# Half-size inverse matrices in a chunked delta rule, the first token group ahead of value and bonuses, and gate products issued inside the last group's norm

## The reference

```python
def wkv7_scan(r, decay, k, v, a_vec, b_vec):        # the delta rule: 8 heads of 64 x 64
    def step(S, inp):
        r_t, w_t, k_t, v_t, a_t, b_t = inp
        sa = jnp.einsum('bhij,bhj->bhi', S, a_t)
        S = (S * w_t[:, :, None, :] + sa[..., None] * b_t[:, :, None, :]
             + v_t[..., None] * k_t[:, :, None, :])
        return S, jnp.einsum('bhij,bhj->bhi', S, r_t)
...
    y = ((y - mean) * lax.rsqrt(var + LNX_EPS)).reshape(bsz, L, RWKV_WIDTH) * lnx_w + lnx_b
    bonus = jnp.sum(rh * kh * r_k, axis=-1, keepdims=True) * vh
    y = (y + bonus.reshape(bsz, L, RWKV_WIDTH)) * g
...
    _, states = lax.associative_scan(s5_combine, (a_elems, bu), axis=1)   # the diagonal model
    y = jnp.real(jnp.einsum('gcp,blgp->blgc', c, states)) + d.astype(f32).reshape(S5_GROUPS, S5_GROUP) * ug
    y = jax.nn.gelu(y.reshape(bsz, L, S5_WIDTH)).astype(u.dtype)
    return y * jax.nn.sigmoid(y @ w_glu + b_glu)
```

## Time and profile before

| | us |
|---|---|
| median of 3 runs | 3404.6 (3401.97 to 3408.07) |
| profiled execution, its own time | 3403.58 |
| its span, first to last instruction | 3402.0 |
| PE busy in the span | 3243.2 (95%) |
| DVE / ACT / POOL busy | 1505.4 / 813.5 / 858.6 |
| mean granted PE clock | 0.986 of full speed |

### The profile page before, as it was taken

How to read it: one execution, slowest core, us unless ns; L and a number is a source line. 1 busy time by engine, 2 the same in 40 slices (tenths; PEclk the granted TensorE clock), 3 DMA queues, 4 the chain that set the end, 5 groups by cost and what they waited for, 6 DMA issues and landing times. The chain is left out here.

```text
span 3402.0 us, 39434 instructions
## 1 busy us (share of the span) xinstructions
PE 3243.2 (95%) x15294; PEld 2320.1 (68%) x15294; DVE 1505.4 (44%) x2685; ACT 813.5 (24%) x1798; POOL 858.6 (25%) x537
## 2 busy tenths in 40 slices
PE   8999999999999999999999999989799999999998
PEld 7857767764444686776666544457587766888886
DVE  5574502331111565646654111143687632655552
ACT  3363301021111344432321111122222121211100
POOL 4314112310000430311003100014255231353352
PEclk9999999999999999999999999999899999999999
DMA  4351221147888322022232688871101122122221
GB/s 154 120 221 50 83 91 75 50 173 288 324 320 309 130 86 88 26 99 106 99 136 99 248 319 324 324 265 75 71 29 54 60 90 99 50 75 95 79 99 50
DMA packets 54206, 470.77 MB, mean 138 GB/s; under 512 B 5888, under 2 KB 10368, under 8 KB 30592
## 3 DMA queue, kind: packets, MB, share of 16 engines
q1 hardware_dynamic: 29040, 379.00, 30.2%
q0 software_dynamic: 21136, 78.39, 5.9%
q10 hardware_dynamic: 3840, 10.75, 0.8%
HBM read 506.65 MB, written 63.18 MB: 167 GB/s over the span
## 5 line engine op out<-in xcount | busy, mean ns | idle before, releaser
L662 PE MATMUL bank<-B,ring 128*128 128x256 f32 x4080 | 900.0, 380 | 17.3 <-DVE B L781 4.4
L662 PEld LDWEIGHTS bank<-B,ring 128*128 128x128 f32 x4080 | 775.7, 191 | 134.7 <-issue 28.4
L646 POOL TENSOR_TENSOR ring<-ring 128x1024 f32<-128x1024 f32 x58 | 148.7, 2563 | 1209.1 <-DMA ring<-in_w_static 378.6
L2095 PE MATMUL bank<-ring,B 128*128 128x512 f32 x960 | 419.1, 594 | 0.3
L812 ACT ACTIVATE B<-bank 128x256 f32<-128x256 f32 x384 | 145.0, 382 | 1022.2 <-PE bank L662 1020.0
L662 PE MATMUL bank<-XT,ring 128*128 128x256 f32 x1472 | 335.2, 382 | 18.9 <-DMA ring<-in_w_static 10.0
L2095 PEld LDWEIGHTS bank<-ring,B 128*128 128x128 f32 x960 | 180.2, 190 | 218.8 <-issue 218.8
L662 PEld LDWEIGHTS bank<-XT,ring 128*128 128x128 f32 x1472 | 280.5, 191 | 64.8 <-issue 17.3
L550 PE MATMUL bank<-B,ring 128*128 128x512 f32 x704 | 305.6, 592 | 4.6 <-DVE B L1496 3.5
L550 PEld LDWEIGHTS bank<-B,ring 128*128 128x128 f32 x704 | 133.5, 190 | 166.0 <-issue 163.9
L2170 DVE TENSOR_TENSOR B<-B,bank 128x512 f32<-128x512 f32 x46 | 31.6, 688 | 468.4 <-PE bank L2095 407.7
(11 more groups left out here) (526 smaller groups left out, 4094.1 us busy)
## 6 DMA issues: line engine op xcount, KB each, us to landing
ring<-in_w_expert SPq DMA_DIRECT2D x96, 2048.0 KB, 9.2
ring<-in_w_static SPq DMA_DIRECT2D x78, 2048.0 KB, 8.5
B<-in_w_expert SPq DMA_DIRECT2D x42, 2048.0 KB
slots_y<-B POOLq DMA_DIRECT2D x52, 512.0 KB, 27.9
B<-slots_x POOLq DMA_DIRECT2D x44, 512.0 KB
slots_x<-B POOLq DMA_DIRECT2D x23, 512.0 KB, 16.2
ring<-s_tables SPq DMA_DIRECT2D x4, 2048.0 KB, 8.4
s_tables<-tmp POOLq DMA_DIRECT2D x8, 512.0 KB, 3.3
```

The costliest lines, as they stand in the source:

```text
L646: pool.tensor_tensor(s(0), w(1, 0), w(1, 1), ALU.add).then_inc(made.up(), 1)
L662: ins = pe.matmul(out, left, right, start=start and k == 0, stop=k == 3, skip_group_check=not start)
L2095: ins = pe.matmul(bank[:, :], xbT[q % 2][:, k, :], slot[:, k, :], start=k == 0, stop=k == KT - 1)
```

## The change

- The inverse uses that chunks of 32 never leave a half of 64 tokens: each head's matrix is kept as two 64 x 64 blocks, one on partitions 0 to 63 and one on 64 to 127. All 8 heads fit one bank. `blockwise` makes 16 products of 64 x 64 where two banks had 4 of 128 x 128 each; squares alternate between two pairs of buffers. L and its transpose share a bank for each `par` (`half_gram`), so does MkT; `mv` and `u` work by halves.
- V is turned in round 2 and not ahead of the round. The shifts of V and the bonuses, `values_and_bonuses`, run in group 0's rounds on DVE; ACT first copies the bonus sums from their banks. Step 1 of the diagonal model moves into group 0, and the steps behind it by two places, so that groups 0 to 3 hold three, four, four and four.
- In pass 4 PE ends the diagonal model's outputs behind chain step 1, ACT makes the gelu there, and the 16 gate matmuls are issued as 3 + 2 + 2 + 9 around the products of the last norm in place of held-clock products. `h_kept` is loaded in group 3.

```diff
+        "above_eye": np.concatenate([near & (at < col), at == col], 1),
         "chunk_upper_incl": same & (i[:, None] <= i[None, :]),
     }
     c = np.stack([tables[n] for n in CONST_NAMES], 1).astype(np.float32)
 
     A, Bh, Kh, Rh = kk, a, k, r
...
-    M, MT, TTr = pair(m.B[0], 4), pair(m.B[0], 6), pair(m.XT, 0)
-    MkT, W1, U = pair(m.XT, 2), pair(m.XT, 4), pair(m.XT, 6)
+    tokB, tokK, tokV = [m.B[0][:, 0, :], m.tmp[:, 3, :]], [m.B[0][:, 1, :], m.rt[:, :]], [m.B[0][:, 2, :], m.XT[:, 2, :]]
+    by_head = lambda t: t.rearrange("p (h i) -> p h i", i=64)
+    fresh = m.B[0][:, 4:6, :].rearrange("p k (h i) -> p k h i", i=64)
+    power = [(fresh[:, 0], fresh[:, 1]), (by_head(m.B[0][:, 6, :]), by_head(m.B[0][:, 7, :]))]
+    MkT, TTr = by_head(m.XT[:, 0, :]), by_head(m.XT[:, 1, :])
+    W1, U = pair(m.XT, 4), pair(m.XT, 6)
...
-    grams = {"L": (A, Bh), "LT": (Bh, A), "MkT": (Kh, A), "NbT": (Bh, Rh), "NkT": (Kh, Rh)}
+    half_grams = {"L": ((A, Bh), (Bh, A)), "MkT": ((Kh, A),)}
+    grams = {"NbT": (Bh, Rh), "NkT": (Kh, Rh)}
...
-                for name in "ABKV":
+                for name in "ABK":
                     plan("tok", tg, name)
-                for name in ("LT", "L"):
-                    for par in range(2):
-                        plan(name, tg, par)
+                for par in range(2):
+                    plan("L", tg, par)
...
                 if tg < TT:
-                    for par in range(2):
-                        if rnd < 4:
-                            plan("sq", tg, rnd, par)
-                        if rnd < 3:
-                            plan("sqT", tg, rnd, par)
-                        if rnd > 0:
-                            plan("tt", tg, rnd, par)
+                    if rnd < 4:
+                        plan("sq", tg, rnd)
+                    if rnd < 3:
+                        plan("sqT", tg, rnd)
+                    if rnd > 0:
+                        plan("tt", tg, rnd)
...
+                if tg < TT and rnd == 2:
+                    plan("tok", tg, "V")
...
+            if tg == TT:
+                plan("glu", 3)
...
-        for j in range(CT):
-            bk.plan(("glu", j), (4, 5)[j % 2])
+        for j in range(3):
+            bk.plan(("glu", j), (*BU_BANKS, SY_BANK)[j])
...
-            feed()
...
+            def half_gram(name, tg):
+                for par in range(2):
+                    pe.wait_ge(*bk.vacant((name, tg, par)))
+                for i, (left, right) in enumerate(half_grams[name]):
+                    for ct in range(4):
+                        for b in range(2):
+                            t, at = slice(tg * P + 64 * b, tg * P + 64 * b + 64), i * 256 + 64 * ct
+                            for par in range(2):
+                                ins = pe.matmul(bk.bank((name, tg, par))[rows(b), at:at + 64], left[rows(par), ct, t], right[rows(par), ct, t],
+                                                start=True, stop=True)
+                                if (i, ct, b) == (len(half_grams[name]) - 1, 3, 1):
+                                    ins.then_inc(bk.full_sem((name, tg, par)), 1)
+
+            def blockwise(key, left, right):
+                pe.wait_ge(*bk.vacant(key))
+                out = by_head(bk.bank(key)[:, :])
+                for head in range(8):
+                    for b in range(2):
+                        ins = pe.matmul(out[rows(b), head, :], left[rows(b), head, :], right[rows(b), head, :], start=True, stop=True)
+                ins.then_inc(bk.full_sem(key), 1)
...
+            def square_round(tg, rnd):
                 if rnd == 0:
...
+                    pe.wait_ge(*bk.vacant(("sq", tg, 0)))
+                    hold_clock(m, pe, bk.bank(("sq", tg, 0)), 7)
+                    pe.wait_ge(*bk.read_done(("L", tg, 0)))
+                    pe.wait_ge(*bk.read_done(("L", tg, 1)))
...
+                M, MT = power[rnd % 2]
                 if rnd < 4:
...
+                    blockwise(("sq", tg, rnd), MT, M)
...
+                    blockwise(("sqT", tg, rnd), M, MT)
...
+                        pe.wait_ge(*bk.read_done(("tt", tg, rnd - 1)))
+                    blockwise(("tt", tg, rnd), M, TTr)
...
+            def gate_products():
+                pe.wait_ge(*m.landed(("glu", 0, 0)))
+                pe.wait_ge(*m.tally("s5_gelu").at(4))
+                for j in range(CT):
+                    pe.wait_ge(*bk.vacant(("glu", j)))
+                    for kt in range(CT):
+                        ins = pe.matmul(bk.bank(("glu", j))[:, :], glu_w[:, kt, j * P:(j + 1) * P], u[:, kt, :], start=kt == 0, stop=kt == CT - 1)
+                        if kt == CT - 1:
+                            ins.then_inc(bk.full_sem(("glu", j)), 1)
+                        yield
+
+            gate_calls = gate_products()
+
+            def fill(n):
+                for _ in range(n):
+                    next(gate_calls, None)
...
                 pe.wait_ge(*bk.vacant(("gm", tg)))
-                if tg == TT - 1:
-                    hold_clock(m, pe, bk.bank(("gm", tg)), 3)
...
-                hold_clock(m, pe, bank, 5)
+                if tg == TT - 1:
+                    fill(2)
+                else:
+                    hold_clock(m, pe, bank, 5)
...
-                    if rnd in (1, 3):
+                    if tg < TT and (rnd == 3 or rnd == 1 and tg):
...
+                        square_round(tg, rnd)
...
+                    if (tg, rnd) == (TT, 1):
+                        for _ in track:
+                            pass
                     if tg < TT:
-                        if rnd < 3:
-                            gram(("MkT", "NbT", "NkT")[rnd], tg)
+                        if rnd == 0:
+                            half_gram("MkT", tg)
+                        if rnd in (1, 2):
+                            gram(("NbT", "NkT")[rnd - 1], tg)
+                        if rnd == 2:
+                            if tg == 0:
+                                pe.wait_ge(*m.tally("shifted_tile").at(len(SHIFTED)))
+                            turned(tg, "V", v)
...
-                                at = (par * 4 + ct) * 64
-                                ins = pe.matmul(bank[:, at:at + 64], MkT[:, par, ct, :], tokV[tg % 2][:, hcol(par, ct)], start=True, stop=True)
+                                head = par * 4 + ct
+                                for b in range(2):
+                                    ins = pe.matmul(bank[rows(b), head * 64:head * 64 + 64], MkT[rows(b), head, :], tokV[tg % 2][rows(b), hcol(par, ct)],
+                                                    start=True, stop=True)
...
+                if tg == TT:
+                    fill(3)
...
+                    pe.wait_ge(*bk.read_done(("tt", tg, 4)))
...
-                            ins = pe.matmul(bank[:, ct * P:(ct + 1) * P], TTr[:, par, ct, :], W1[:, par, ct, :], start=True, stop=True)
+                            for b in range(2):
+                                ins = pe.matmul(bank[rows(b), ct * P:(ct + 1) * P], TTr[rows(b), 4 * par + ct, :], W1[rows(b), par, ct, :],
+                                                start=True, stop=True)
...
-            for _ in track:
-                pass
-            pe.wait_ge(*m.landed(("glu", 0, 0)))
-            pe.wait_ge(*bk.vacant(("glu", 0)))
-            hold_clock(m, pe, bk.bank(("glu", 0)), 7)
...
-                project(m, pe, ("glu", j), lambda kt, c: glu_w[:, kt, c * P:(c + 1) * P], j, CT, lambda kt: u[:, kt, :])
+            fill(4 * CT)
...
+            for j in range(CT):
+                evict(("bo", j), bonus[:, j, :], lambda b: b[:, :])
...
+                        M, MT = power[(rnd + 1) % 2]
+                        if rnd == 1:
+                            act.wait_ge(*m.tally("first_inverse").at(tg + 1))
+                        evict(("sq", tg, rnd), M, lambda b: by_head(b[:, :]))
+                        if rnd < 3:
+                            evict(("sqT", tg, rnd), MT, lambda b: by_head(b[:, :]))
+                        if rnd == 2:
+                            evict(("tok", tg, "V"), tokV[tg % 2], lambda b: b[:, :])
...
+                    if tg == TT - 1:
+                        act.dma_start(m.B[0][:, :, :], m.dram["h_kept"]).then_inc(m.restored, 16)
...
+                if tg == TT:
+                    for c in range(4):
+                        act.wait_ge(*bk.read_done(("sy", c)))
+                        act.activation(u[:, c, :], u[:, c, :], ACT.Gelu_apprx_tanh).then_inc(m.tally("s5_gelu").up(), 1)
+                    act.activation(m.v[:, 63:64], m.small[:, ROW_EPS], ACT.Sqrt)
...
-            act.dma_start(m.B[0][:, :, :], m.dram["h_kept"]).then_inc(m.restored, 16)
             act.dma_start(m.XT[:, :, :], m.dram["x_kept"]).then_inc(m.restored, 16)
-            for c in range(4):
...
-            shift(3)
-            dve.wait_ge(*m.tally("shifted_tile").at(len(SHIFTED)))
...
-            for j in range(CT):
-                dve.wait_ge(*bk.made(("bo", j)))
```

(54 more changed lines are left out.)

103 lines of the change are left out of this document (32 added, 71 removed).

## The result

The changed kernel takes 3377.0 us (median of four runs, 3373.4 to 3380.6) against 3404.8 (3402.0 to 3408.1, four runs): a ratio of 0.9918, 95% interval 0.9901 to 0.9935. The forecast was 3371, with 3352 to 3394 as its range. The profiled execution took 3373.7 us.

The account below looks back on a forecast made before the run. PE's order of work sets the pace in groups 0 to 3, DVE nearly so, DVE before them, a chain of small steps at the end: -19.4 - 7.5 - 7.5 - 6.9 + 14.3 - 6.3 = -33.3, giving 3371 us, range 3352 to 3394.

Parts of the forecast that it names:

- 1. The rounds, and group 3: Groups 1 to 3: smaller products and less DVE work save 7.5 us each in groups 1 and 2, 6.9 in group 3.
- 2. The start: Ahead of and in group 0: transposes start 18.1 us earlier, group 0 itself gains 1.3, so group 1 starts 19.4 earlier.
- 3. The clock: Sign against the forecast, in the groups' rounds: it would be wrong if PE's granted clock there is below 1.
- rival (e): Rounds: the half-empty array lets PE's clock fall, slower; 3437 us if half the new work runs at half speed; chance 0.08.
- 4. What is late next: Last chain and outputs: PE waits about 5.8 us for POOL's late end of step 15; +14.3 us in all (8 to 18).
- the low clock: Last chain: after PE's gap for POOL, some 6 us of work at half speed, +2.9 us.
- the stall of 1.8: Last chain: a second weight transfer can hold PE's instructions as in group 3, half of 3.6, +1.8 us.
- 5. The tail: After the last outputs: gate products issued around the norm's products cut 24.8 us to 18.5, a gain of 6.3.
- (b): Small things go well: no stall or low clock in the last chain, faster small products, group 3 without gap; 3356 us; chance 0.15.
- (c): DVE becomes the bound: three groups save 5.2 in place of 7.5, group 0 saves 7 less; 3385 us; chance 0.13.
- (d): Small products run one behind the other, `blockwise` 1.76 us, so the rounds gain nothing on PE; 3398 us; chance 0.05.
- the other signs that were to show the forecast wrong: No DVE waits in groups 1 to 3, V tiles at 3.3 us each, or DVE closing the last chain's gap early.

Follow-up runs that it names:

- e5: Changed kernel with value and bonuses back ahead of group 0 and the gate products back behind the last norm, leaving chiefly the half-size matrices: 3376.1 us.
- e1: Changed kernel with the state's sum kept in PSUM, so the multiplication by the decay reads one SBUF input: 3368.3 us.
- e6: Changed kernel with only the move of value and bonuses undone: they come ahead of group 0 again, gates stay moved: 3370.4 us.
- after: The changed kernel itself, with the whole change and no further edit: 3377.0 us.
- e2: Changed kernel with POOL's six products of a diagonal-model step on 8 columns in place of 512, leaving POOL nearly idle: 3347.4 us.
- e4: Changed kernel with the diagonal model's last products on PE moved from behind the last chain's first step to behind its fourth: 3370.6 us.
- e3: Kernel before the change with POOL's six products of a diagonal-model step cut to 8 columns in place of 512: 3395.9 us.
- e10: Kernel e6 (value and bonuses ahead of group 0) with the edits of e1 and e4 added: 3372.6 us.

## Why the prediction was right, and where it was not

The direction, the median within 6 us, and the order of what is late next came out. The nearness of the median is in part luck: by the stages of the mixer the forecast was -33.3 us and the profiles show -24.5; the spans differ by 29.9 because 5.7 more lie ahead of the change. By its own steps, in stage sums:

**1. The rounds, and group 3: the mis-sized term.** Forecast -7.5, -7.5 and -6.9; measured -4.2, -1.9 and -5.3, so -11.4 in place of -21.9. The price of the new products was not at fault. `blockwise` costs 0.96, below my 1.15, and half-size matrices by themselves save 26.9 us in the three groups (e5). What failed is that I priced the rounds as if nothing else of the change touched them. The move of value and bonuses shifts the diagonal model's steps, and in groups 1 and 2 one multiplication of the state each is then held up by POOL's products: 6.18 and 3.97 us instead of 0.42 (e1 takes 9.7 us from these two groups, e6 13.9; the 4.2 between them are not traced). I had seen the long forms of the earlier trace rows beside POOL and used them for the shifted tiles alone, and the 3.79 us of the kernel before I had not seen.

**2. The start.** Forecast -18.1, measured -18.4: the working holds. For group 0 I forecast -1.3 and -0.3 came out, but that is luck. It was made of -7.5 for the rounds and +6.2 for the exchange of a model step against values and bonuses. The runs show -0.4 for the first (e5: PE's saving went into waits, 5.7 us of them for POOL's sums) and +0.5 for the second (*after* against e6). The one wait that I had priced, for the bank of NbT's product at 1.2 us, was longer:

```profile
2455.66 2.08 PE L2602 MATMUL bank<-B 64*128 64x128 f32 x16 [4.61 <-DVE XT L3226]
```

**3. The clock.** I named a granted clock below 1 in the rounds as what would prove me wrong; it is 0.87 and 0.91 in groups 1 and 2. It was not the half-empty array of rival (e): with the same small products and no load on POOL it is 0.94 and 0.96 (e2), with POOL's load and the values in their old place 0.97 and 0.94 (e6), near the 0.95 and 1.00 of the kernel before in the earlier trace rows.

**4. What is late next.** Forecast +14.3, measured +11.8. POOL ends 19.9 us after the norm product (19.3 to 20.4 forecast), PE waits 5.21 (5.8), and from chain step 2 to the end of the outputs it is 7.1 (7.1). The model's outputs took 3.63 us instead of 2, at a granted clock of 0.55 from the end of PE's wait to chain step 2, so step 2 started at 24.7 instead of 22.5. So the low clock, priced at 2.9 us for the work behind, fell on these outputs; from step 2 on the clock was 1.00, and the stall of 1.8 did not come. e4 confirms the mechanism.

**5. The tail.** Forecast -6.3; measured -6.2 (18.8 us against 18.5 forecast).

**By parts of the change.** Added up by part, the forecast gave the half-size matrices -29.4 us (-7.5, -7.5, -7.5, -6.9), the gates -6.3, and value and bonuses +2.4 (-18.1, +6.2, +14.3): by its own terms that move did not pay, which I did not notice. Measured are -27.6 (e5 against before), -5.1 (e6 against e5) and +8.2 (*after* against e6).

**The rivals.** (b) was right on the prices of the products (`blockwise` 0.96 us against its 0.9, the 32 products of `half_gram` 1.09 against 1.0 at its four-position rate), and not on what they bring. (c), DVE the bound, is nearest to what happened but in its reason wrong: DVE's work fell by 4.0 us in group 1 without POOL's load (43.56 in e3, 39.61 in e2) and by 8.8 with it (49.96 before, 41.16 in e5), where 5.2 was forecast, and the large losses came where it was held up. (d) is out: 16 products in one bank start within 0.96 us, where one behind the other would take 1.76. (e) is out, as above. Of the other signs that were to show the forecast wrong, none came: DVE had waits in groups 1 to 3, and of the four tiles of V only one had a long first pass (1.75 us).

What stays open: how a two-input instruction is held up over several POOL products in a row. In e6 a multiplication beside POOL's products took 0.44 us while POOL's product took 1.46 instead of 1.27. Who yields is not settled by these runs. Open too is the cause of the 2.8 us by which G1 differs between executions.

## What to carry to other kernels

Price a moved piece of work by what it shifts on every other engine, not only by the gap that it leaves: here the move of 18 us of vector work cost some 27 us elsewhere, and the half-size matrices alone (e5) were as fast as the whole change. When the busiest engine gets lighter, look next at the longest form of each short instruction of the second one; hold-ups that were free in the groups before (e3: none shorter by more than 0.9 us) become the path. A vector instruction with two SBUF inputs on the critical chain is worth a try with one of them in PSUM if GpSimd works beside it: here that gave 8.7 us where the instruction was held up (e1); in e10, where it was not, it gave nothing, together with e4's edit.

## What the runs showed of the hardware that I had not expected

- A vector multiplication of 128 x 256 from two SBUF inputs took 6.18 us beside five back-to-back GpSimd products, 3.97 in the next group, and 6.18 and 3.98 again in e4; elsewhere beside such products it took 0.44 (e6); from PSUM and SBUF it took 0.423 to 0.426 us sixteen times in sixteen.
- Sixteen fp32 products of 64 x 64 on two diagonal positions of the array, all into one bank, start to next start: 0.96 us, less than twice the 0.61 us of eight.
- The kernel before could drop nearly all of POOL's work in the mixer and its groups 1 to 3 stayed at 179.4 us instead of 179.6; the changed kernel's went from 168.2 to 147.5.
